# One activation table for the roots; cross attention woven into its query projections and into the output projection of tile 0

## The reference

```python
def rmsnorm(x, g):                       # also per head, in the mixer
    return x * rsqrt(mean(x * x) + 1e-6) * g

mem_n = rmsnorm(mem, mem_norm_g)         # (256, 1024)
x = x + hybrid_mixer(rmsnorm(x, ...))    # forgetting attention | HGRN2 | conv, then @ w_out
x = x + cross_attention(rmsnorm(x, ...), mem_n, w_xq, w_xkv, w_xo)
x = x + hierarchical_moe(rmsnorm(x, ...))
return rmsnorm(x, final_norm_g)

def cross_attention(h, mem_n, w_xq, w_xkv, w_xo):      # 4 heads of 256
    q = h @ w_xq;  k, v = split(mem_n @ w_xkv)
    s = q @ k.T / 16;  p = softmax(s);  o = p @ v
    return o @ w_xo

def hierarchical_moe(h, ...):            # 4 groups x 4 experts, hidden 256
    # the best group of a token, its 2 best experts, weights from two softmaxes
    # out += (silu(h @ w_gate) * (h @ w_up) * weight) @ w_down
```

## Time and profile before

| | |
|---|---|
| median of 3 runs | 714.07 us |
| the profiled execution | 712.32 us |
| its span (first to last instruction) | 710.3 us |
| PE busy | 681.3 us (96%) |
| DVE, ACT, POOL busy | 280.6, 153.2, 78.5 us |
| chain that ended last | 87% PE |
| DMA | 111.90 MB |
| mean granted clock of PE | 0.996 |

### The profile page before, as it was taken

One profiled execution on the slowest core, in us unless ns is written; L12 is line 12 of the kernel. 1 busy time (PEld: TensorE's weight loads), 2 busy tenths in 40 slices (PEclk: granted clock), 3 DMA queues, 4 the chain that ended last, 5 costly groups with the idle time before them and its releaser, 6 DMA issues.

```text
span 710.3 us, 8420 instructions
## 1 busy us (share of the span) xinstructions
PE 681.3 (96%) x3398; PEld 331.4 (47%) x3398; DVE 280.6 (40%) x669; ACT 153.2 (22%) x315; POOL 78.5 (11%) x106
## 2 busy tenths in 40 slices
PE   7999999999999999999999999999999999999993
PEld 4644445453547665444444446545565333333331
DVE  3107599927034665213220006513334821212156
ACT  3011351003273444211000104301211010101112
POOL 3000081402020000000000000000001011110062
PEclk9999999999999999999999999999999999999998
DMA  8803240303036513300019406030029999999763
GB/s 288 308 0 119 82 154 1 119 1 108 15 119 180 178 60 119 118 1 0 1 36 395 161 0 237 0 119 30 30 87 341 363 372 389 376 375 392 268 219 137
DMA packets 69939, 111.90 MB, mean 158 GB/s; under 512 B 5648, under 2 KB 43780, under 8 KB 69900
## 3 DMA queue, kind: packets, MB, share of 16 engines
q1 hardware_dynamic: 65724, 96.16, 39.1%
q0 software_dynamic: 4176, 15.21, 5.8%
HBM read 101.90 MB, written 9.46 MB: 157 GB/s over the span
## 4 chain that ended last, share of the span: by engine, by line
PE 87%; DMA 4%; DVE 3%; ACT 3%; issue 1%; POOL 1%; SPq 0%; DVEq 0%; POOLq 0%; ACTq 0%
PE bank L1917 26%; PE bank L2193 16%; PE bank L1792 11%; PE bank L1927 6%; PE bank L1821 5%; PE bank L2263 2%; PE bank L1963 2%; PE bank L2243 2%; PE bank L2146 2%; PE bank L1949 2%; DMA W<-y_dram,A 2%; PE bank L1774 1%; PE bank L2124 1%; PE bank L2133 1%; PE bank L2035 1%; DMA x_sb<-in_x_dram 1%
## 5 line engine op out<-in xcount | busy, mean ns | idle before, releaser
L1917 PE MATMUL bank<-hT,W 128*128 128x512 f32 x368 | 159.7, 593 | 0.9 <-DVE hT L1071 0.9
L2193 PE MATMUL bank<-W,n_sb 128*128 128x512 f32 x256 | 114.2, 596 | 0.7 <-ACT n_sb L1039 0.7
L1917 PEld LDWEIGHTS bank<-hT,W 128*128 128x128 f32 x368 | 69.4, 190 | 87.5 <-issue 86.0
L1792 PE MATMUL bank<-W,A 128*32 128x512 f32 x672 | 84.8, 594 | 1.5 <-DVE A L1162 1.5
L2193 PEld LDWEIGHTS bank<-W,n_sb 128*128 128x128 f32 x256 | 47.1, 190 | 53.9 <-issue 52.3
L1425 DVE SCALAR_TENSOR_TENSOR A<-A,pc 128x511 f32<-128x511 f32 (+29 forms) x60 | 51.6, 860 | 2.0
L695 POOL TENSOR_TENSOR rstd<-ss,mhalf 128x1 f32<-128x1 f32 x14 | 7.7, 550 | 367.6 <-DVE ss L1055 203.1
L1792 PEld LDWEIGHTS bank<-W,A 128*32 128x32 f32 x672 | 23.1, 110 | 49.6 <-issue 47.6
L1821 PE MATMUL bank<-Dn,A 128*32 128x512 f32 x264 | 36.3, 595 | 0.0
L906 ACT ACTIVATE A<-bank 128x512 f32<-128x512 f32 (+1 forms) x22 | 12.1, 556 | 103.7 <-PE bank L1917 77.0
L1277 DVE TENSOR_TENSOR A<-A,bank 128x256 f32<-128x256 f32 x12 | 5.1, 421 | 71.7 <-ACT A L825 71.7
(11 more groups left out here) (306 smaller groups left out, 818.5 us busy)
## 6 DMA issues: line engine op xcount, KB each, us to landing
W<-in_w_gate_dram SPq DMA_DIRECT2D x14, 1024.0 KB, 13.3
W<-in_w_up_dram SPq DMA_DIRECT2D x14, 1024.0 KB, 14.5
Dn<-in_w_down_dram SPq DMA_DIRECT2D x11, 1024.0 KB, 13.8
W<-in_w_in_dram SPq DMA_DIRECT2D x5, 2048.0 KB, 9.3
W<-in_w_xkv_dram SPq DMA_DIRECT2D x4, 2048.0 KB, 8.3
hT<-in_w_down_dram SPq DMA_DIRECT2D x5, 1024.0 KB, 12.7
y_dram<-A POOLq DMA_DIRECT2D x10, 512.0 KB, 7.1
W<-in_w_out_dram SPq DMA_DIRECT2D x2, 2048.0 KB, 8.0
```

What stands on the lines that cost most here:

```text
L1792: mm = nc.tensor.matmul(PS[2 + b][r, :], xgT[:, b, c, r], gu_at[GU_HOME[e]][:, c, :], start=c == 0, stop=c == DC - 1)
L1917: mm = nc.tensor.matmul(bank[0:w, 0:n], lhs, src[:, c, 0:n], start=c == 0, stop=c == DC - 1)
L2193: mm = nc.tensor.matmul(PS[k % 4][:, :], src[:, c, t * P:(t + 1) * P], W[:, (n_load + n) % SLOTS, c, :], start=first and j == 0, stop=last ...
```

## The change

1. ACT loads one table that holds both Ln and Exp ahead of the first roots.
2. The memory's first turned tile is evacuated by DVE ahead of the HGRN2 norm; the second tile's transposes stand inside the last value group, after its 4th and 6th matmul.
3. The queries go to banks 2 and 3. After query groups 0 and 1, the scores of head 0 start; later groups alternate with scores, turnings and products of the heads. In the last head, where no query is left, matmuls of the output projection of tile 0 take that place. The scores of a head wait for its own two query groups alone.
4. The output projection's banks move by two, so that tile 0 has banks 2 and 3. The router's loop starts at tile 1, and takes both turnings and both halves of the logits of tile 0 there. VectorE's order in the router is as before.
5. VectorE makes two maxima and then two normings, not one of each in turn.
6. `turn_late` stands in passes 2 and 4 (before 2 and 3), its copy in passes 3 and 5 (before 3 and 4).

```diff
--- before.py
+++ after.py
@@ -460,7 +460,7 @@
         def bank_of(g):
 
 
-            return g % 4 if g < 16 else 7 if XKV0 <= g < XQ0 - 1 else g % 2
+            return g % 4 if g < 16 else 7 if XKV0 <= g < XQ0 - 1 else 2 + g % 2 if g >= XQ0 else g % 2
 
         def bank_free(pe, g):
 
@@ -944,6 +944,7 @@
             ho_evac(0)
             proj_evac(22, 23)
             act.wait_ge(consts, 2)
+            nc.scalar.preload_act_table_set("natural_log_exp_and_others")
             for c in range(2):
                 act.wait_ge(cvar, c + 1)
                 inv_root(c, PS[4 + c][:, :], croot[c], crs)
@@ -1018,7 +1019,7 @@
                 act.wait_ge(x1_done, 2 * t + 2)
                 square(act, 2, t, x_sb, junk[:, t % 2])
             kv_evac(XQ0 - 1)
-            for c in range(DC):
+            def x_query(c):
                 g = XQ0 + c
                 act.wait_ge(proj, g + 1)
                 nc.scalar.activation(xqT[:, c], PS[bank_of(g)][:, :], ACT.Copy).then_inc(proj_out, 1)
@@ -1038,12 +1039,21 @@
                     act.wait_ge(xo_ps, g + 1)
                     nc.scalar.activation(xoT[:, g], PS[6 + n][:, :], ACT.Copy).then_inc(xo_sb, 1)
 
-            for h in range(XH + 1):
-                if h < XH:
-                    for t in range(ST):
-                        x_exp(h * ST + t)
+            x_query(0)
+            for h in range(XH):
+                if h < XH - 1:
+                    x_query(2 * h + 1)
+                elif h:
+                    x_query(DC - 1)
+                for u in range(h * ST, h * ST + 2):
+                    x_exp(u)
+                if h < XH - 1:
+                    x_query(2 * h + 2)
                 if h >= 1:
                     x_out(h - 1)
+                for u in range(h * ST + 2, h * ST + 4):
+                    x_exp(u)
+            x_out(XH - 1)
             experts_act(act)
 
 
@@ -1100,7 +1110,7 @@
             def add_half(t, n):
                 dve.wait_ge(wout_ps, 8 + 2 * t + n + 1)
                 xs = x_sb[:, t, 512 * n:512 * n + 512]
-                nc.vector.tensor_tensor(xs, xs, PS[(2 * t + n) % 4][:, :], ALU.add).then_inc(x1_done, 1)
+                nc.vector.tensor_tensor(xs, xs, PS[(2 * t + n + 2) % 4][:, :], ALU.add).then_inc(x1_done, 1)
 
             def first_mean(t):
                 dve.wait_ge(sq_done, NORM0[3] + 2 * t + 1)
@@ -1293,8 +1303,8 @@
                     y_half(p - 1)
                 if p == 1:
                     late_rows()
-                if 3 <= p < 3 + LATE:
-                    late_turned(p - 3)
+                if p in (3, 5):
+                    late_turned(p // 2 - 1)
 
             def add_row(k, t, w):
                 dve.wait_ge(fin_in[t][k], 16)
@@ -1529,6 +1539,8 @@
 
             for t in range(MT):
                 normed(dve, 1, t, mem_sb, mem_sb)
+            for k in range(2):
+                turn_evac(dve, 1, 0, k, PS[6 + k], memT, R_MEM)
             for p in range(HP):
                 dve.wait_ge(ho_rs, p + 1)
                 nc.vector.scalar_tensor_tensor(out=hob[p], in0=hob[p], scalar=pc[:, R_HG + p:R_HG + p + 1],
@@ -1536,8 +1548,8 @@
                 dve.wait_ge(ho_step, 2 * p + 1)
                 nc.vector.tensor_tensor(catT[:, 4 + p], hob[p], hgT[:, p], ALU.mult).then_inc(ho_step, 1)
 
-            for k in range(2 * MT):
-                turn_evac(dve, 1, k // 2, k % 2, PS[6 + k % 2], memT, R_MEM)
+            for k in range(2):
+                turn_evac(dve, 1, 1, k, PS[6 + k], memT, R_MEM)
 
 
             def f_scores(u, a):
@@ -1651,16 +1663,13 @@
                         dve.wait_ge(xo_ps, 2 * (h - 1))
                     nc.vector.tensor_copy(xpT[:, g % 4], PS[4 + m][:, :]).then_inc(xpt_sb, 1)
 
-            for h in range(XH + 1):
-                for t in range(ST):
-                    if h < XH:
-                        x_max(h * ST + t)
-                        if t >= 1:
-                            x_norm(h * ST + t - 1)
-                    if t == 1 and h:
-                        x_pt(h - 1)
-                if h < XH:
-                    x_norm(h * ST + ST - 1)
+            for h in range(XH):
+                for t in range(0, ST, 2):
+                    x_max(h * ST + t)
+                    x_max(h * ST + t + 1)
+                    x_norm(h * ST + t)
+                    x_norm(h * ST + t + 1)
+                x_pt(h)
             experts_dve(dve)
 
         def turn_group(pe, stage, t, k, bank, src):
@@ -1733,23 +1742,22 @@
                     if t == ST - 1 and c % 4 == 3:
                         mm.then_inc(xt_ps, 1)
 
-            for q in range(2):
-                loaded(pe, 14 + q)
             pe.wait_ge(router_in, 16 * 4)
             pe.wait_ge(router_const, 8)
-            for t in range(ST):
+            for t in range(1, ST):
                 first, middle, rest = range(2), range(2, 5), range(5, DC)
                 project_some(8, 14, xoT, 2 * t, first, last=False)
-                if t:
-                    turn_half(t - 1, 1)
+                if t == 1:
+                    turn_half(0, 0)
+                turn_half(t - 1, 1)
                 project_some(8, 14, xoT, 2 * t, middle, first=False, last=False)
-                if t:
-                    logits_half(t - 1, 1)
+                if t == 1:
+                    logits_half(0, 0)
+                logits_half(t - 1, 1)
                 project_some(8, 14, xoT, 2 * t, rest, first=False)
                 project_some(8, 14, xoT, 2 * t + 1, first, last=False)
                 turn_half(t, 0)
-                if t:
-                    position(t - 1, range(t))
+                position(t - 1, range(t))
                 project_some(8, 14, xoT, 2 * t + 1, middle, first=False, last=False)
                 logits_half(t, 0)
                 if t == ST - 1:
@@ -1860,8 +1868,8 @@
 
                     pe.wait_ge(ht_sb, p)
                 turn_hidden(p % 2, ht_ps)
-                if 2 <= p < 2 + LATE:
-                    turn_late(p - 2)
+                if p in (2, 4):
+                    turn_late(p // 2 - 1)
             down_pass(NP - 1)
 
             pe.wait_ge(over_done, 1)
@@ -2108,10 +2116,16 @@
             pe.wait_ge(ho_sb, HP)
             for k in range(2):
                 turn_group(pe, 1, 0, k, PS[6 + k], mem_sb)
-            g = run([along(1, 3, 0, FW)], g, 5)
-            for k in range(2):
-                pe.wait_ge(turn_sb, TURN0[1] + k + 1)
-                turn_group(pe, 1, 1, k, PS[6 + k], mem_sb)
+            def last_values(bank):
+                for c in range(DC):
+                    if c in (4, 6):
+                        k = c // 2 - 2
+                        pe.wait_ge(turn_sb, TURN0[1] + k + 1)
+                        turn_group(pe, 1, 1, k, PS[6 + k], mem_sb)
+                    mm = nc.tensor.matmul(bank[:, 0:FW], hT[:, c, 3 * P:4 * P], W[:, 1, c, 0:FW], start=c == 0, stop=c == DC - 1)
+                return mm
+
+            g = run([last_values], g, 5)
 
 
             def qk(u):
@@ -2190,7 +2204,7 @@
                 if k >= 4 and first:
                     pe.wait_ge(x1_done, base + k - 3)
                 for j, c in enumerate(chunks):
-                    mm = nc.tensor.matmul(PS[k % 4][:, :], src[:, c, t * P:(t + 1) * P], W[:, (n_load + n) % SLOTS, c, :],
+                    mm = nc.tensor.matmul(PS[(k + (2 if base else 0)) % 4][:, :], src[:, c, t * P:(t + 1) * P], W[:, (n_load + n) % SLOTS, c, :],
                                           start=first and j == 0, stop=last and j == len(chunks) - 1)
                 if last:
                     mm.then_inc(wout_ps, 1)
@@ -2231,12 +2245,12 @@
             project_out(0, 10, catT, order + [3], 2, begun=3)
             pe.wait_ge(turn_sb, TURN0[3])
             pe.wait_ge(x1_done, 8)
-            g = run([across(0, P * c) for c in range(4)], g + 1, 12)
-            g = run([across(1, P * c) for c in range(4)], g, 13)
-            pe.wait_ge(proj_out, GROUPS_END)
+            def x_query(c):
+                run([across(c // 4, P * (c % 4))], XQ0 + c, 12 + c // 4)
 
             def x_scores(u):
                 h, t = divmod(u, ST)
+                pe.wait_ge(proj_out, XQ0 + 2 * h + 2)
                 if u >= 2:
                     pe.wait_ge(xe_done, u - 1)
                 for k in range(2):
@@ -2264,15 +2278,36 @@
                                               xpT[:, (2 * h + m) % 4, :], start=m == 0, stop=m == 1)
                     mm.then_inc(xo_ps, 1)
 
-            for h in range(XH + 1):
-                for t in range(ST):
-                    if h < XH:
-                        x_scores(h * ST + t)
-                    if t == 1 and h:
-                        x_turn(h - 1)
+            def out_some(k, chunks, first):
+                pe.wait_ge(xo_sb, chunks[-1] + 1)
+                project_some(8, 14, xoT, k, chunks, first=first, last=chunks[-1] == DC - 1)
+
+            x_query(0)
+            for h in range(XH):
+                x_query(2 * h + 1)
+                if h:
```

(21 more changed lines are left out.)

## The result

The changed kernel takes 706.62 us (median of 4 runs, 706.44 to 707.01). The kernel before, with one run more on the same chip, takes 713.95 (4 runs, 712.83 to 714.19). The ratio is 0.9902, 95% interval [0.9886, 0.9918]: faster by 1.0%, and by more than the forecast said (708.6). It lies 0.6 us under the low end of my range of 8 in 10 (707.2).

What follows compares the result with a forecast made beforehand. The prediction took PE to bound the kernel, with 87% of the chain. Its terms, 2.75 + 3.6 - 1.7 + 1.1 - 0.3 = 5.5 us, came off 714.07 to give 708.6; range of 8 in 10: 707.2 to 711.0.

Steps and rivals of the forecast that it cites:

- The memory's turning: Between the last value group and the next key projection, all 2.75 us of PE's idle time go.
- Cross attention: From the last query to the output projection PE idles 4.3 us; 0.7 stays at the first scores, 3.6 go.
- The thin cover of 0.88 against 0.7: Cross attention, heads 1 to 3: the second query's copy (0.7 us) hides beside the former head's turning (0.88 us).
- The router's wait: At the router's start, tile 0's second turning waits for DVE's add: PE idles 1.7 us more.
- The late turning: In the expert passes, PE's idle 1.13 us until DVE's copy in pass 3 goes: 1.1 us gained.
- The weights: Expert passes, tightest at pass 10: waiting for weight transfers returns 0.3 us; as rival, all 1.1 lost, 709.4 us, chance 0.13.
- no wait at the scores of heads 1 to 3: Denies a rival: in cross attention the queries' copies aren't covered, three heads give back 0.7 us each, 710.7; chance 0.07.
- one router wait and not four: Denies a rival: the router's wait comes at each tile, three more of 1.7 us, 713.7; chance 0.04.
- no load between the roots: Denies a rival: compiler keeps table loads between the roots, 1.5 us gained instead of 2.75, 709.9; chance 0.01.
- The rival: PE's clock falls at the router's start, where a 1.7 us stop is added; ten matmuls slowed give 717.4 us; chance 0.03.

Runs made afterwards that it cites:

- one half of the change alone: Kernel before with only the new order of the memory's turning, table loads between the roots left in; 711.43 us, ratio 0.9972.
- the late turning alone: Kernel before with only `turn_late` moved to passes 2 and 4 and its copy to passes 3 and 5; 711.90 us, ratio 0.9976.
- the weaving alone: Kernel before with only parts 3, 4 and 5 of the change; 711.11 us, ratio 0.9960.
- filled: Kernel before with two constant matmuls added, one in each of PE's two stops at the memory's turning; 712.12 us, ratio 0.9980.
- with one stop: Two kernels, each the kernel before with one part: only the new order of the memory's turning, 711.43 us; only the table load ahead of the roots, 711.47 us.
- the last two: Changed kernel with both DVE adds of tile 0 first, 704.67 us; the same plus one matmul of query group 2 ahead of the first scores, 704.21 us.
- lengthened: Kernel before with a net two more table loads between ACT's two roots, making the stop at the memory's turning longer; 717.69 us, ratio 1.0064.
- the control's: Kernel before, unchanged, timed again beside the kernel before; 713.59 us, ratio 1.0000.

## Why the prediction was right or wrong

**The memory's turning: right.** 2.75 forecast, 2.75 by the starts. PE itself is what is late there, as the working said, and with one half of the change alone 1.45 were gained where I had 1.5.

**Cross attention: right.** 3.6 forecast. From the key projection to the first pass 1.8 us are gained by the anchors; with the router's 1.7 added back this is 3.5. The thin cover of 0.88 against 0.7 held: in this stage PE's waits have one entry, 0.7, and it is that of the first scores.

**The router's wait: right**, 1.7 forecast, 1.72 by starts (1.56 as listed), and its cause is shown by the kernel in which DVE adds first.

**The late turning: right, a little small.** 1.1 forecast. The pass behind it starts 6.53 earlier and that before it 4.78 earlier (572.96, 568.18), which is 1.75; but the second transposes moved to the next pass and take 0.43 of it back there (598.65, 592.55, or 6.10 earlier). It is 1.3. Alone it gave 1.4 in the medians.

**The weights: right.** 0.3 forecast, 0.2 listed at pass 10, where I had put it. None of the other rivals came: no wait at the scores of heads 1 to 3, one router wait and not four, no load between the roots.

So the sum of 5.5 stands against 5.9 between the two profiled executions, and the 706.8 for the profiled execution against 706.44. Of the 0.4, 0.2 each are the late turning and the earlier start of the mixer's projections.

**The step that failed is the last sentence of the sum:** "The median of the runs is 1.75 above the profiled one, so I forecast 714.07 - 5.5 = 708.6." I took over the distance between the median and the trace of before as if it belonged to any kernel. It belongs to the kernel before and to its first three runs: the changed kernel has medians at 0.2 and 0.1 above its profiled executions. Of the miss of 2.0 us this step is 1.6, and the sum the other 0.4.

What the 1.75 were made of is known in part. 75 runs of the kernel before on three chips have a median of 713.3, so 0.8 was the luck of three runs (or of the chip they ran on). The rest, 1.0 above the profiled execution, can be split by the clock:

| 75 runs of before | runs | median us |
|---|---|---|
| mean clock 0.993 or less | 22 | 714.8 |
| mean clock above 0.993 | 53 | 712.8 |

The two groups are 2.0 us apart, near the 1.7 by which the key group was longer in the trace with the fall. The long ones lift the median of all from 712.8 to 713.3, by 0.5. The last 0.5, from 712.32 to 712.8, no run explains. Against the medians after (706.6 and 706.9) the runs above 0.993 give 6.0 us, near the 5.9 of the traces, and all runs give 6.5. So the clock accounts for about 0.5 us of the miss, less than the luck of the first runs: three of the four stood at 713.8 or more, which put the distance at 7.3.

**The reading of the clock failed too, with a smaller part.** I wrote that "between 205 and 215, PE was busy for 7.78 of 10 us in two stops, and the granted clock was 1.00 of full", and took that as evidence against a fall. It was one execution, and one in which the clock held. The rival had the right mechanism in the wrong kernel: I priced a clock that falls where the change adds a stop, and did not ask whether it falls already where the change removes one. In the traces here the router's 1.56 us did not bring it down. The share of runs at 0.993 or less follows the stops at the turning: 22 of 75 and, with the late turning alone, 4 of 12 where both are there, but 0 of 6 with the weaving alone; 0 of 12 filled; 0 and 1 of 12 with one stop; 1 of 23 with none (the kernel with parts 1 and 2, the changed one twice, and the last two); 6 of 6 lengthened.

The Trainium skill, in TensorE: Matmul & The Clock Gate, section "A second HAM failure mode: psum-queue depth-cycling", tells of a bf16 kernel whose short stops between groups of matmuls, on banks that are used in turn, bring the clock down again and again. I had said that the trace didn't bear it out. For three of the traces with both stops, that of before, the control's and that of the weaving alone, this stays so; for that of the late turning alone (0.60 from 216 to 219) it doesn't.

**Open.** Why the clock falls in some executions of the same program and not in others isn't known. The fall itself was seen in two traces only, since each kernel leaves one; for all other runs it is inferred from the mean clock. The limit of 0.993 is mine, read from where the runs part, and it can't be clean. In the traces the clock also goes to 0.50 when PE has ended its last matmul, and the moment varies: from 700 to 705 us it is 0.97 in the profiled execution of before and 0.70 in the control's, so the first has a mean of 0.996 and the second of 0.994 though neither fell at the turning. That costs no time, since PE has nothing left to do. The fall in the trace of the late turning takes 1.7 of 710 us, or 0.002 of the mean, as much as lies between these two ends. So a run at 0.994 can hide a fall, and one at 0.993 need not have one at this place: one of the 23 without a stop stands there. Which property of the stretch brings the fall wasn't separated either: in the 3.63 us between the value group's end and the key projection PE does nothing but the eight transposes, and no run kept the two stops with other work between them. Runs spread by 1 us and more at either clock.

## What to carry to other kernels

Take a sum worked out in one trace off that trace's time (712.32 - 5.5 = 706.8 was 0.2 from the median of 706.62), and before carrying it to a median of three runs, look at more runs, their spread and their mean clocks: the distance may be chance, or what lifts some runs may be what the change removes. A stop of a few us of PE can cost more than itself (2.5 us beside the longer stop), and one trace at full clock doesn't show that it never does. Where a change makes an engine wait for two results instead of one, write out the other engine's order between them; moving one add ahead was worth the whole wait.

## What the runs showed of the hardware

- With stops of 1.23 and 0.99 us and 1.25 of transposes between them, 22 of 75 executions of the kernel before have a mean clock of 0.993 or less. With 3.81 and 0.99, all 6 do, and in the trace the clock is at 0.50 from 216 to 222, a stretch in which PE is busy for 5.01 of 6 us.
- The clock comes back while PE works: in the trace of the late turning alone it is 0.60 from 216 to 219 us and 1.00 from 219 to 222, with PE busy for 3.00 and 2.77 of 3 us.
- After PE's last matmul the clock goes to 0.50 (705 to 710 us in the traces of before and of its control). A mean clock over the whole execution holds this too.
- Two constant matmuls that stand in the stops cost nothing in the trace (10.50 us before and after), and with them 0 of 12 runs have a mean clock of 0.993 or less.
- Ln and Exp of 128x512 from one table follow each other: four in 2.6 us. With their four loads they took from 202.32 to 210.22, 7.9; the 5.3 more are 1.3 for each load, which is the load's own 1.28. The Trainium skill, in ScalarE: Activation LUTs, section "What ACT_TABLE_LOAD costs", puts a drain of 1.38 us beside each load of 1.28, and so 2.66 for a change of table. No such drain shows in this trace; the measured 1.3 decides.
